# Stick-breaking attention walked by chunks of 512 keys, and constant score rows read with the keys, in a hybrid decoder layer

## The reference, cut to what matters

```python
# stick-breaking, for every head; strictly causal
z = q @ k.T / sqrt(64)
log_keep = where(s < t, log_sigmoid(-z), 0)
after = reversed_cumsum(log_keep) - log_keep
w = where(s < t, exp(log_sigmoid(z) + after), 0)
o_sb = w @ v
# softmax heads: q and k normed, the last 32 columns rotated; causal
o_mla = softmax(q @ k.T / sqrt(96)) @ v
# both multiplied by a SiLU gate, side by side, then
out = x + gate * (concat(o_sb, o_mla) @ w_out)
```

## Time and profile before

| | |
|---|---|
| median of 3 runs | 2027.88 us (2025.8 to 2030.19) |
| the profiled execution's own time | 2028.02 us |
| its span | 2026.3 us, 31777 instructions |
| mean granted TensorE clock | 0.969 |
| TensorE busy | 1870.7 us (92%) |
| VectorE busy | 1238.1 us (61%) |
| GpSimd busy | 1034.0 us (51%) |
| ScalarE busy | 948.1 us (47%) |
| DMA | 273.83 MB, mean 135 GB/s |

### The profile page before, as it was taken

One profiled execution on the slowest core, in us unless ns is written; L12 is line 12 of the kernel. 1 busy time (PEld: TensorE's weight loads), 2 busy tenths in 40 slices (PEclk: granted clock), 3 DMA queues, 4 the chain that ended last, 5 costly groups with the idle time before them and its releaser, 6 DMA issues.

```text
span 2026.3 us, 31777 instructions
## 1 busy us (share of the span) xinstructions
PE 1870.7 (92%) x9669; PEld 1533.2 (76%) x9669; DVE 1238.1 (61%) x1864; ACT 948.1 (47%) x1889; POOL 1034.0 (51%) x1041
## 2 busy tenths in 40 slices
PE   6899999979999997499998989899999999987998
PEld 1687888858999996277776767678788887876786
DVE  1643222125555556498989989878988889872010
ACT  1431111123333333277776767567777777771000
POOL 2520000001333334099898989967878878771222
PEclk9899999989999999599999999989999999998999
DMA  7397533334556553831706335424252544415654
GB/s 270 117 321 235 178 99 99 124 115 163 182 178 198 186 178 133 204 66 38 192 23 151 79 85 124 106 71 84 64 123 62 129 83 82 147 42 156 190 184 146
DMA packets 224772, 273.83 MB, mean 135 GB/s; under 512 B 13936, under 2 KB 161680, under 8 KB 219264
## 3 DMA queue, kind: packets, MB, share of 16 engines
q1 hardware_dynamic: 220736, 265.53, 46.3%
q10 hardware_dynamic: 3904, 6.82, 1.1%
HBM read 159.06 MB, written 109.05 MB: 132 GB/s over the span
## 4 chain that ended last, share of the span: by engine, by line
PE 25%; issue 14%; POOL 8%; DVE 7%; DMA 3%; ACT 2%; SPq 1%; POOLq 0%; DVEq 0%; ACTq 0%
PE at_high L2212 8%; DVE sb_w L1638 4%; PE at_low L2175 3%; POOL sb_wh L1532 3%; PE at_b L2228 3%; PE at_b L2229 2%; PE at_low L1724 2%; POOL sb_wl L1534 2%; DMA out_x<-in_x 2%; POOL out_o L2347 2%; POOL wl L2008 1%; PE at_b L1753 1%; PE at_b L2240 1%; PE at_b L1768 1%; PE at_b L1769 1%
## 5 line engine op out<-in xcount | busy, mean ns | idle before, releaser
L2008 POOL TENSOR_TENSOR wl<-w,wh 128x512 fp32r<-128x512 f32 (+1 forms) x320 | 378.6, 1199 | 98.8 <-ACT wh L2035 93.2
L1534 POOL TENSOR_TENSOR sb_wl<-sb_wf,sb_wh 128x512 fp32r<-128x512 f32 (+2 forms) x240 | 289.3, 1205 | 19.2
L1638 DVE TENSOR_TENSOR_SCAN sb_w<-kp,sb_w,at_high 128x512 f32<-128x512 f32 x192 | 245.5, 1279 | 28.2 <-ACT kp L1560 12.9
L2034 ACT ACTIVATE w<-at_high 128x512 f32<-128x512 f32 (+1 forms) x320 | 170.8, 534 | 113.9 <-PE at_high L2212 56.6
L2087 DVE TENSOR_REDUCE nmx<-at_low 128x1 f32<-128x512 f32 (+2 forms) x320 | 191.8, 601 | 7.5 <-PE at_low L2175 4.5
L604 PE MATMUL pt_po<-h_hi,pt_wh 128*128 128x512 f32 x448 | 177.5, 396 | 9.7 <-issue 6.8
L1560 ACT ACTIVATE kp<-at_low 128x512 f32<-128x512 f32 (+3 forms) x320 | 168.8, 531 | 32.5 <-PE at_low L1727 11.6
L606 PE MATMUL pt_po<-h_hi,pt_wl 128*128 128x512 f32 x448 | 179.5, 401 | 0.0
L605 PE MATMUL pt_po<-h_lo,pt_wh 128*128 128x512 f32 x448 | 177.9, 397 | 0.0
L1532 POOL CAST sb_wh<-sb_wf 128x512 fp32r<-128x512 f32 (+2 forms) x240 | 142.5, 594 | 55.7 <-ACT sb_wf L1571 51.1
L2035 ACT ACTIVATE wh<-at_high 128x512 fp32r<-128x512 f32 (+1 forms) x320 | 169.1, 528 | 0.0
(11 more groups left out here) (246 smaller groups left out, 4582.7 us busy)
## 6 DMA issues: line engine op xcount, KB each, us to landing
qk_mla<-tk_th SPq DMA_DIRECT2D x64, 192.0 KB, 2.1
qk_mla<-tk_tl SPq DMA_DIRECT2D x64, 192.0 KB, 2.3
whole<-in_w_ada SPq DMA_DIRECT2D x4, 2048.0 KB, 18.5
pt_w<-in_w_feat SPq DMA_DIRECT2D x16, 512.0 KB, 5.8
qk_sb<-pt_oh SPq DMA_DIRECT2D x32, 256.0 KB, 3.5
qk_sb<-pt_ol SPq DMA_DIRECT2D x32, 256.0 KB, 4.4
hT<-h_hi SPq DMA_DIRECT2D x16, 512.0 KB, 5.1
hT<-h_lo SPq DMA_DIRECT2D x16, 512.0 KB, 6.1
```

Source lines behind the costliest of these rows:

```text
L1534: nc.gpsimd.tensor_tensor(wl[i][:, lo:GW], wf[i][:, lo:GW], wh[i][:, lo:GW].bitcast(F32), ALU.subtract).then_inc(s_plo, 1)
L1638: nc.vector.tensor_tensor_scan(kept, keeps, beside[:, 0:b - a], 1.0 if u["n"] == 0 else w[u["g"]][:, u["r"], b:b + 1], ALU.mult, ALU.bypas ...
L2008: nc.gpsimd.tensor_tensor(wl[i][:, cols], w[i][:, cols], wh[i][:, cols].bitcast(F32), ALU.subtract).then_inc(s_lo, 1)
```

## The change

`Plan` orders a group by chunks of 512 keys from the right to the left: the four tiles of queries against one chunk, then the next chunk. A turn needs only its own chunk, so turn x stands in the slot of unit x + 7 (`LEAD`), and 7 turns are left at the end of a pair. The four buffers `sb_w` hold one chunk each (8 KB a partition, 112 KB to 144 KB); a chunk's first running product waits for the turns of the chunk four before. The 20 pieces of the softmax part are spread over the 7 left turns. The first load of keys is split in two. The scratch tensor `qk_mla` gets a 97th row with the constants, stored in `tokens` by three DMAs; `keys`, `q_lo` and `k_lo` are loaded with 97 rows each time, `q_hi` with 96, and the six writes of constants go. `k_lo` of head 0 no longer waits for the last units; the four loads of head 1 stand behind the store of group 3 and the load of gate 1.

```diff
@@ tokens
+            sp.wait_ge(s_even, 2)
+            for which, l, i in ((1, 0, 1), (0, 1, 0), (1, 1, 0)):
+                sp.dma_start(qkS[which, l, :, QK, :].rearrange("n (c p) -> n c p", p=P),
+                             even[i][0:NB, :].unsqueeze(1).broadcast_to([NB, H, P])).then_inc(s_evenst, 16)
-                    sp.dma_start(qkS[which, l, j, :, half * HH * P:(half + 1) * HH * P],
+                    sp.dma_start(qkS[which, l, j, 0:QK, half * HH * P:(half + 1) * HH * P],
...
+            for i in range(2):
+                nc.gpsimd.memset(even[i][:], float(i)).then_inc(s_even, 1)
@@ Plan
-    SHIFT = sum((NB - r) * P for r in range(QG)) + 4 * GW
+    LEAD = 7
+    TILES = 4
...
+                for c in reversed(range(g + 1)):
+                    chunk = len(self.units) // QG
+                    for r in range(QG):
+                        a, z = c * GW, min((c + 1) * GW, (g * QG + r + 1) * P)
+                        self.units.append(dict(head=head, g=g, r=r, a=a, z=z, n=g - c, chunk=chunk))
+                    for j in range(c * QG, (c + 1) * QG):
...
+        for x in range(T):
+            self.slots[(x + self.LEAD) % U].append((x, (x + self.LEAD) // U))
@@ attend_sb, sync
-        for at in range(2):
-            sp.dma_start(buf["kk"][0][at * HD:(at + 1) * HD, :].bitcast(F32), qk[at, H * HD:H * HD + HD, :]
-                         ).then_inc(s_first, 16)
+        for cols, sem in ((late, s_first), (slice(0, late.start), s_keys)):
+            for at in range(2):
+                sp.dma_start(buf["kk"][0][at * HD:(at + 1) * HD, cols].bitcast(F32), qk[at, H * HD:H * HD + HD, cols]
+                             ).then_inc(sem, 16)
...
                 softmax.load_v(sp, 0, 0)
-                sp.wait_ge(s_z, PAIRS * U)
-                sp.wait_ge(s_t, it * T + plan.groups[GROUPS]["turns"])
                 softmax.load_qk(sp, 0, 0, ("kl",))
-                softmax.load_qk(sp, 0, 1, ("qh", "kh", "ql", "kl"))
             for g in (3, 2):
                 store(it, g)
                 load_gate(it, g - 2)
+                if last and g == 3:
+                    sp.wait_ge(s_z, PAIRS * U)
+                    softmax.load_qk(sp, 0, 1, ("qh", "kh", "ql", "kl"))
@@ attend_sb, vector
-            if u["r"] == 0 and u["n"] == 0:
-                reached(dve, s_t, it * T + plan.turns_through(plan.rows[u["row"]]["group"] - GROUPS))
+            if u["r"] == 0:
+                reached(dve, s_t, it * T + (u["chunk"] - TILES + 1) * QG)
             if u["n"] > 0:
-                dve.wait_ge(s_scan, it * U + n)
+                dve.wait_ge(s_scan, it * U + n - QG + 1)
@@ attend_sb, tensor
-            if tn["first"]:
-                pe.wait_ge(s_scan, it * U + plan.groups[tn["group"]]["units"])
+            if tn["starts"]:
+                pe.wait_ge(s_scan, it * U + (tn["chunk"] + 1) * QG)
@@ attend_mla, load_qk
-                sp.dma_start(dst[hp][0:QK, :].rearrange("p (n c) -> p n c", n=NB).bitcast(F32),
-                             qkS[which, l, :, :, col].rearrange("n p c -> p n c")).then_inc(sem[hp], 16)
+                rows = QK if name == "qh" else KP
+                sp.dma_start(dst[hp][0:rows, :].rearrange("p (n c) -> p n c", n=NB).bitcast(F32),
+                             qkS[which, l, :, 0:rows, col].rearrange("n p c -> p n c")).then_inc(sem[hp], 16)
@@ Memory, build
-        self.sb_w = [tile(f"sb_w{g}", [P, QG, (g + 1) * GW], o * K) for g, o in ((0, 136), (1, 120), (2, 96), (3, 64))]
+        self.sb_w = [tile(f"sb_w{i}", [P, QG, GW], (112 + 8 * i) * K) for i in range(4)]
-    qk_mla = scratch("qk_mla", (2, 2, NB, QK, H * P))
+    qk_mla = scratch("qk_mla", (2, 2, NB, QK + 1, H * P))
```

More of the change, by code:

```diff
@@ L668, in tokens @@
         dv = m.sb("dv", [P, H * HD])
+        even = [m.sb(f"even{i}", [P, P]) for i in range(2)]
         vt = m.sb("vt", [P, H, 2, HD], F32R)
@@ L728, in tokens @@
         s_ident = m.sem("ident")
+        s_even = m.sem("even")
+        s_evenst = m.sem("evenst")
         s_const = m.sem("const")
@@ L1294 @@
 class Plan:
-    SHIFT = sum((NB - r) * P for r in range(QG)) + 4 * GW
+    LEAD = 7
     RING = 4
+    TILES = 4
     def __init__(self):
-        self.units, self.rows, self.turns, self.groups = [], [], [], []
+        self.units, self.turns, self.groups = [], [], []
         for head in range(2):
             for g in reversed(range(GROUPS)):
[L1311 to L1326, removed]
@@ new lines, in __init__ @@
+                group, first_turn = len(self.groups), len(self.turns)
+                for c in reversed(range(g + 1)):
[4 more added lines that the diff above has]
+                    for j in range(c * QG, (c + 1) * QG):
+                        self.turns.append(dict(group=group, head=head, g=g, j=j, lowest=max(0, j - g * QG), chunk=chunk,
+                                               at=(j - c * QG) * P, starts=(j == c * QG),
+                                               first=(j == g * QG), last=(j == QG - 1)))
@@ L1327, in __init__ @@
+                self.groups.append(dict(head=head, g=g, turn0=first_turn, turns=len(self.turns), units=len(self.units)))
         U, G, T = len(self.units), len(self.groups), len(self.turns)
-        self.U, self.G, self.T, self.R = U, G, T, len(self.rows)
+        assert U == T and U // QG % self.TILES == 0
+        self.U, self.G, self.T = U, G, T
         self.slots = [[] for _ in range(U)]
-        ends = []
-        for u in self.units:
-            ends.append((ends[-1] if ends else 0) + u["z"] - u["a"])
@@ L1360, in due @@
         return [(n, when // self.T) for n, when in ends if when % self.T == x]
-    def turns_through(self, group):
-        return self.groups[group]["turns"] if group >= 0 else self.groups[group + self.G]["turns"] - self.T
 def attend_sb(nc, m, mem, banks, qk, vS, gates, mix):
     plan = Plan()
-    U, T, R, G = plan.U, plan.T, plan.R, plan.G
+    U, T, G = plan.U, plan.T, plan.G
     PAIRS = H // 2
-    RING = plan.RING
+    RING, TILES = plan.RING, plan.TILES
     PTS = 3
@@ L1698, in vector @@
             slot(PAIRS, [turned])
-            softmax.maxima_ahead(dve, i)
+            softmax.maxima_ahead(dve, i, len(plan.rest))
         for x in range(AFTER + 5):
@@ L1715, in unit @@
                 pe.wait_ge(s_first, 96)
+            elif n == QG and isinstance(it, int):
+                pe.wait_ge(s_keys, 32)
             elif n in (0, plan.groups[0]["units"] if isinstance(it, int) else 0, U // 2):
@@ L1753, in turn @@
                 tp = nc.tensor.transpose(pt[x % PTS][:, r * P:(r + 1) * P],
-                                         w[tn["g"]][:, r, tn["j"] * P:(tn["j"] + 1) * P], ident[:])
+                                         w[tn["chunk"] % TILES][:, r, tn["at"]:tn["at"] + P], ident[:])
             tp.then_inc(s_t, 1)
@@ L1790, in tensor @@
             slot(PAIRS, [turned])
-            softmax.pieces_ahead(pe, i)
+            softmax.pieces_ahead(pe, i, len(plan.rest))
         for x in range(T - LAG, T):
@@ L1796, in attend_sb @@
         keep, scan, z, t = (s_keep, PAIRS * U), (s_scan, PAIRS * U), (s_z, PAIRS * U), (s_t, PAIRS * T)
-        widest = (s_t, (PAIRS - 1) * T + plan.groups[GROUPS]["turns"])
         whole = (s_whole, PAIRS * plan.pooled_to(T - 1))
@@ L2072, in scalar, with ahead @@
         run(act, dict(row=row, turn=weights, half=v_low, sums=totals, mh=high), lambda x: output.split_high(act, x))
[L2074 to L2081, removed]
+    def ahead(i, of):
+        return range(i * AHEAD // of, (i + 1) * AHEAD // of)
     def maxima(dve):
@@ L2097, in maxima, with maxima_ahead @@
         return dict(piece=maximum, nm=row_maximum)
[L2099 to L2107, removed]
+    def maxima_ahead(dve, i, of):
+        for p in ahead(i, of):
+            turn_of(-1, 1, T - AHEAD + p, maxima(dve))
     def vector(dve, output):
@@ L2181, in pieces, with pieces_ahead @@
         return dict(piece=piece)
-    def pieces_ahead(pe, i):
-        if i < AHEAD:
-            turn_of(-1, 1, T - AHEAD + i, pieces(pe))
+    def pieces_ahead(pe, i, of):
+        for p in ahead(i, of):
+            turn_of(-1, 1, T - AHEAD + p, pieces(pe))
     def tensor(pe, output):
@@ L2264, in attend_mla @@
         stored = [(s, 16 * G * PAIRS) for s in s_st]
-    return Softmax(sync, gpsimd, scalar, vector, tensor, done, load_qk, load_v, rows_ahead, maxima_ahead, pieces_ahead)
+    return Softmax(sync, gpsimd, scalar, vector, tensor, done, load_qk, load_v, maxima_ahead, pieces_ahead)
 def output(nc, m, mem, banks, stick, softmax, t, keep, mix_sb, mix_mla, out, s_wout):
```

12 lines of the change are left out of this document (6 added, 6 removed).

## The result

| | before | after |
|---|---|---|
| median | 2028.61 us (2025.8 to 2030.19, 4 runs) | 2553.64 us (2552.06 to 2555.31, 4 runs) |
| ratio, 95% interval | | 1.259 (1.2568 to 1.2612) |
| span of the profiled execution | 2026.3 us | 2553.6 us |
| mean granted TensorE clock | 0.969 | 0.869 |

The forecast was 2679 us with a range of 2400 to 3060. The direction and the mechanism held, and the size was 125 us too large. Of all executions behind this document one was slow: 3667.54 us, one of the six with 98 rows (experiment 3), and the ratios leave it out.

The account below looks back on a forecast made before the run. VectorE and GpSimd together were taken to bound stick-breaking, TensorE the softmax stage. With 97-row loads on one engine, p = 43.5 us each, the span was 1633 + 24p = 2677 us, plus 1.7: 2679 us, range 2400 to 3060.

Parts of the forecast that it names:

- part 1: Stick-breaking's order by chunks: minus 22 + 3 - 2 + 12 = minus 9 us, between minus 21 and plus 37.
- a fifth between ends of 0 and 58: Stick-breaking: narrow units in fours unbalance VectorE and GpSimd; 58 us if nothing were elastic, a fifth taken, 12 us.
- One engine for 97 rows: Loads of `keys`, `q_lo`, `k_lo`: 97 is prime, so all 1552 packets go to one engine; at about 28 ns, chance 0.60.
- p: Time of one 97-row load on one engine: 1552 packets x 28 ns = 43.5 us, ends 31.8 and 58.4 us.
- The chain: SyncE's queue: three such loads a head, 130 us against 62 us of computing, delay all behind them; span 2677 us.
- Z: Time when half of the last stick-breaking pair is scored: 1226 us before, 1237 us forecast afterwards.
- B0: Landing of head 1's loads in the first softmax pair, 6 + 3p after head 0's; gate 0 comes only behind it.
- the step from A to B: Softmax pairs: from landing of head 0's loads to head 1's, 14 us + 3p in later pairs, for SyncE's group 2 store.
- even deal: Rival: 97-row loads stay on 16 engines and hidden, only the chunk order counts: 2019 us, 2007 to 2065; chance 0.14.
- Slow packets: Rival: one engine, but the pitch of `qk_mla` makes packets slow, 58.4 us a load: 3037 us; chance 0.20.
- fast packets: Rival: one engine at the best slices' pace, 31.8 us a load: 2398 us; chance 0.06.
- No shorter tail: Rival: GpSimd falls behind in diagonal chunks, stick-breaking's tail stays: alone 2028 to 2065 us; no chance of its own.

Follow-up runs that it names:

- experiment 3: Changed kernel with 98 rows instead of 97 in `qk_mla` and the three loads, the added row unused: 2020.27 us, ratio 0.9962.
- split kernel: Changed kernel with each load of `keys`, `q_lo` and `k_lo` as two DMAs, rows 0 to 95 and row 96 alone: 2020.33 us, ratio 0.9964.
- experiments 1 and 8: Changed kernel with row 96 in a DMA of its own, loaded each time (1: 2020.33 us) or only once a buffer (8: 2020.19 us).

## Why the prediction was right or wrong

**The bound now, and the order by chunks: right.** I forecast minus 9 us for part 1 alone, 2019 us; the split kernel took 2020.33. Its pieces, from the kernel with the row loaded once, by tile (first and last start) and in TensorE's timeline (first score of the softmax part, after it that of the kernel before):

```profile
L1635 DVE TENSOR_TENSOR_SCAN sb_w<-kp,at_high x128: 384/804/1222, 835.6 to 1291.3; 128x128 f32<-128x128 f32 x32, 128x256 f32<-128x256 f32 x32, 128x384 f32<-128x384 f32 x32, 128x512 f32<-128x512 f32 x32
L1531 POOL TENSOR_TENSOR sb_wl<-sb_wf,sb_wh x240: 723/1284/1647, 843.1 to 1307.1; 128x512 fp32r<-128x512 f32 x88, 128x256 fp32r<-128x256 f32 x16, 128x384 fp32r<-128x384 f32 x16
1317.78 0.76 PE L2202 MATMUL at_high<-q_hi,keys 97*128 97x512 f32 x1 [0.45 <-ACT q_hi L2042]
1325.37 0.77 PE L2212 MATMUL at_high<-q_hi,keys 97*128 97x512 f32 x1 [0.45 <-ACT q_hi L2041]
```

The start came 2.3 us earlier (forecast 2), though in the profile of the changed kernel itself it stands at 837.9 us as before, so the 2 us aren't sure. The running products last 457 us against 445, 12 longer; I had 15, of which 12 were a guess of a fifth between ends of 0 and 58, so this term was met in part by luck. GpSimd's end trails theirs by 16 us as forecast (15), but then 9 us pass to the first softmax score, against 4 before. From the last running product to the first score it is 25 us against 42, minus 17 where I had minus 22. The pieces give minus 7 us, the ratio of the split kernel too; the two small errors nearly cancel.

The sum had no term for TensorE's clock in this tail. Windows from 1300 us on in the kernel before, with the row loaded once and LEAD 7, and with LEAD 9 (the columns of the earlier trace rows):

```profile
1300.00:1308.00 8.00, 5.59 (x37) 4.43 (x35) 6.49 (x9) 3.58 (x6) 7.72 (x8) 1.00 0.26 86
1300.00:1308.00 8.00, 7.34 (x20) 4.86 (x18) 4.57 (x8) 0.88 (x2) 4.50 (x6) 0.50 0.82 199
1300.00:1308.00 8.00, 6.11 (x30) 4.38 (x30) 7.19 (x13) 2.34 (x5) 4.66 (x7) 1.00 0.90 212
```

With LEAD 7 TensorE runs here at a granted clock of 0.50, the 1.2 GHz level, and is busy for 7.34 of 8 us; with LEAD 9 it has the full clock (2.4 GHz), and the first score stands at 1314.54 us, 3 us earlier. So the tail's missing 5 us go together with the lower clock. LEAD 9 changes the left turns too, so it is no test of that. What makes the clock fall is open: from 1292 to 1300 us TensorE was busy for 5.07 of 8 us with LEAD 7 and 6.46 with LEAD 9, but in the kernel before, which kept its clock, for 5.25.

**Constants by DMA: right**, nothing (experiments 1 and 8).

**One engine for 97 rows: right**, shown by the times and flows of 97, 98 and 106 rows.

**One load: the term that was mis-sized.** I took 28 ns a packet, from the fastest flow of such packets on sixteen engines, and gave 20.5 ns as the other end. One engine alone does it in 23.4 ns, p = 36.3 and not 43.5 us. Over 24 loads that is 173 us too much. The argument (fifteen others less at the memory) went the right way and not far enough: 28 ns still was a price with sixteen engines at work. The landing spacing of 36.3 us is off the 43 us that I had named as the sign for p.

**The chain: right in form, 49 us short.** The two errors have opposite signs, so the total is nearer than p alone would have made it. Z was 1237.66 us, forecast 1237. With p = 36.3 the sum's 1633 + 24p is 2504 us, and the span was 2553.6:
- Gate 0 landed at 1472.8 us, 3 later than the sum has it (B0 + 2 is 1470 with this p).
- Head 0 was scored at 1533.84, 61 us after gate 0 and not 47: plus 14. The failed step is "head 0 does eight turns and waits". It did none. ScalarE writes the row maximum of head 0 (L2039) behind the last `mh` of stick-breaking, and that waits for VectorE in front of gate 0: TensorE's row of 110.1 us above. I had looked at VectorE's queue behind the gate and not at ScalarE's.
- To the loads of the next head 129.4 us, forecast 124: plus 5.
- Two periods of a pair took 252.6 and 250.2 us, forecast 6p + 24 = 242: plus 19. It lies in the step from A to B, 134.4 and 133.2 us where 3p + 14 is 123: the turns up to the store of group 2 run only after an idle time, at a granted clock of 0.50 in it (1885 to 1900 us) and 0.78 behind it (1900 to 1916 us). How much of the step the clock makes was not tested.
- From the last loads' issue to the first score of the last head 116.7 us, forecast 114: plus 2; the head itself 61 and not 55: plus 6; the output projection 2 less.

That makes 47 of the 49 us.

**The rivals.** The even deal fell, and its time came true where the loads are dealt evenly. "Slow packets" fell: one engine alone takes 23.4 ns a packet from `qk_mla` and not 37.6, so this pitch doesn't slow an engine alone. Why sixteen engines get 218 GB/s from `qk_mla` and 295 from `v_mla` stays open. For one load "fast packets" was nearer the truth than the middle (31.8, 36.3 and 43.5 us), but in the total the middle was nearer, as the chain was short. "No shorter tail" fell in part: the tail is shorter, and two thirds of that is paid back before it. The chances of the four cases add up to 1 by themselves, so there was no room for the remainder of 0.04 that I named.

**What stays open.** Why the running products last 12 us longer in the order by chunks is argued from the pairing of narrow units with full turns, not shown: moving the sigmoid forward moved the waits without a gain, and LEAD 9 for 7 makes a difference of 1 us (5 with the sigmoid forward). More buffers between the engines weren't tried.

## What to carry to other kernels

Count the rows of a DMA before adding one: a constant that rides along "for free" as the 97th row cost 525 us, while the same row in a DMA of its own, or one useless row more, costs nothing that shows. When issues on a queue grow and the DMA's share in a stretch with such loads alone is near one sixteenth (7.2% here), look for a count of rows that can't be dealt evenly, and look who stands behind it in the queue: here an unchanged load and two gates paid too. The version to keep is the order by chunks with 96-row loads, the constant row loaded once a buffer, and LEAD 9: 2018.88 us, ratio 0.9959 (0.9945 to 0.9972) to the kernel before. Its time can't be told from that of LEAD 7.

## What was not expected of the hardware

In these traces one engine moves 512 B packets at 22 GB/s, one in 23.4 ns, alone or with a second one beside it; with sixteen at work on the same tensor each gets 13.6 GB/s (218 in all). So moving all packets to one engine costs ten times (36.3 against 3.5 us) and not sixteen times the time. When it was empty, the queue let SyncE go at once from two of these loads and held it at the third: 0.36, 0.69 and 3.61 us before, 0.33, 0.59 and 37.32 us here. What it counts isn't shown; the second load, 1552 packets for one engine, held SyncE for only 0.59 us. At the third, with one engine loaded and fifteen empty, it held SyncE about as long as that one engine needed.
